# Compressed first-layer product of the second mixer on four column tiles, two chunks a step

## The reference, cut to what matters

```python
n_cmp = (T - CMP_LEN) // CMP_STRIDE + 1            # 15
blk = x[:, cmp_idx] + pe[None, None, :, None, :]
blk = jnp.transpose(blk, (0, 1, 3, 2, 4)).reshape(B, n_cmp, G, CMP_LEN * Dh)   # 2048 wide
hid = jax.nn.gelu(jnp.einsum('bngi,ih->bngh', blk, w1))                        # w1: 2048 x 256
return jnp.einsum('bngh,ho->bngo', hid, w2)                                    # w2: 256 x 64
```

## Time and profile before

| | us |
|---|---|
| median of 3 runs | 1629.38 |
| lowest, highest | 1627.42, 1630.9 |
| the profiled execution, its own time | 1627.93 |
| its span, first to last instruction | 1626.1 |
| PE busy in the span | 1592.5 |
| DVE busy | 951.4 |
| ACT busy | 802.6 |
| POOL busy | 167.1 |

### The profile page before, as it was taken

How to read it: one execution, slowest core, us unless ns; L and a number is a source line. 1 busy time by engine, 2 the same in 40 slices (tenths; PEclk the granted TensorE clock), 3 DMA queues, 4 the chain that set the end, 5 groups by cost and what they waited for, 6 DMA issues and landing times.

```text
span 1626.1 us, 22861 instructions
## 1 busy us (share of the span) xinstructions
PE 1592.5 (98%) x8768; PEld 1368.9 (84%) x8768; DVE 951.4 (59%) x1454; ACT 802.6 (49%) x1358; POOL 167.1 (10%) x187
## 2 busy tenths in 40 slices
PE   9999999999999999999999999999999989999997
PEld 7888899888888888888899988888888878878886
DVE  5555575444765555555456544665554778577865
ACT  6444465454364445444355454454443555453653
POOL 1000022211200000000022221120000301010100
PEclk9999999999999999999999999999999999999999
DMA  7665455443555554655546443446565453245421
GB/s 253 204 211 204 148 191 171 143 142 126 160 182 183 192 188 162 207 181 184 188 152 196 146 139 127 146 153 218 197 215 191 150 190 107 78 154 171 146 85 52
DMA packets 76718, 269.60 MB, mean 166 GB/s; under 512 B 8512, under 2 KB 9792, under 8 KB 76608
## 3 DMA queue, kind: packets, MB, share of 16 engines
q1 hardware_dynamic: 76320, 267.35, 49.4%
q10 hardware_dynamic: 288, 0.79, 0.1%
HBM read 267.06 MB, written 1.05 MB: 165 GB/s over the span
## 4 chain that ended last, share of the span: by engine, by line
PE 72%; DVE 5%; ACT 4%; issue 2%; POOL 1%; DMA 0%; POOLq 0%; DVEq 0%; ACTq 0%
PE bank L1433 20%; PE bank L1435 20%; PE bank L1434 20%; PE bank L1439 4%; PE bank L1558 2%; PE bank L1573 2%; DVE wlo L2281 1%; DVE cv L2278 1%; PE bank L1690 1%; ACT hh L1971 1%; ACT wk L2203 1%; PE bank L1500 1%; PE bank L1496 1%; PE bank L1492 1%; ACT whi L1968 1%
## 5 line engine op out<-in xcount | busy, mean ns | idle before, releaser
L2281 DVE TENSOR_TENSOR wlo<-raw,whi 128x1024 fp32r<-128x1024 f32 (+5 forms) x472 | 564.6, 1204 | 406.0 <-ACT whi L1968 370.4
L1968 ACT ACTIVATE whi<-raw 128x1024 fp32r<-128x1024 f32 (+4 forms) x500 | 508.9, 1029 | 426.4 <-PE bank L1435 394.6
L1433 PE MATMUL bank<-whi,hh 128*128 128x512 f32 (+3 forms) x1120 | 434.4, 388 | 0.0
L1435 PE MATMUL bank<-whi,hl 128*128 128x512 f32 (+3 forms) x1120 | 425.3, 380 | 0.0
L1434 PE MATMUL bank<-wlo,hh 128*128 128x512 f32 (+3 forms) x1120 | 424.8, 379 | 0.0
L1435 PEld LDWEIGHTS bank<-whi,hl 128*128 128x128 f32 x1120 | 210.5, 188 | 38.5
L1434 PEld LDWEIGHTS bank<-wlo,hh 128*128 128x128 f32 x1120 | 210.9, 188 | 35.9
L1433 PEld LDWEIGHTS bank<-whi,hh 128*128 128x128 f32 x1120 | 210.8, 188 | 35.6
L1433 PE MATMUL bank<-hh,whi 128*128 128x256 f32 x480 | 142.0, 296 | 0.0
L1433 PE MATMUL bank<-whi,gh 128*128 128x512 f32 x352 | 139.4, 396 | 0.0
L1435 PE MATMUL bank<-whi,gl 128*128 128x512 f32 x352 | 138.0, 392 | 0.0
(11 more groups left out here) (326 smaller groups left out, 1887.2 us busy)
## 6 DMA issues: line engine op xcount, KB each, us to landing
raw<-W SPq DMA_DIRECT2D x463, 512.0 KB, 3.3
raw<-W SPq DMA_DIRECT2D x26, 384.0 KB, 3.7
raw<-W SPq DMA_DIRECT2D x8, 416.0 KB, 3.0
tab<-tab SPq DMA_DIRECT2D x6, 384.0 KB, 4.0
raw<-W SPq DMA_DIRECT2D x4, 426.0 KB, 3.4
raw<-W SPq DMA_DIRECT2D x6, 192.0 KB, 2.6
x<-x_in SPq DMA_DIRECT2D x2, 512.0 KB, 6.5
tab<-gains SPq DMA_DIRECT2D x2, 512.0 KB, 4.9
```

What stands on the lines that cost most here:

```text
L1433: e.matmul(dst, ah, bh, start=start, stop=False)
L1435: return e.matmul(dst, al, bh, start=False, stop=stop)
L1968: return e.activation(dst, src, ACT.Copy)
L2281: return e.tensor_tensor(dst, src, hi.bitcast(F), ALU.subtract)
```

## The change

- `m2_cmp` takes two chunks a step. Each of a chunk's four slices goes to a column tile of its own, 32 columns of weights and all 256 hidden columns streaming. The tiles sum over different slices, so that PSUM holds 4 x 32 rows (four partial sums) x 256 per kv: a whole bank of 128 x 512.
- `m2_hid_copy` (new, on ACT) copies this bank to SBUF (`hid4`), and the bank is given back.
- `m2_hid_sum` (new, on PE): four f32 matmuls, with 128 columns of `hid4` as weights and a 128 x 30 matrix of zeros and ones (`K_SEL`) streaming. They add the four parts and turn the result at once, into 128 x 120.
- The gelu steps work on 128 x 120 rather than 64 x 256 and write `hid`; `m2_turn_hid` goes, and the factor 0.5 moves to the copy in `m2_cmp_out`.
- `tiles()` has four calls fewer, and the pace of `tick()` goes from 22/54 to 18/54.

```diff
-                for q in range(4):
-                    c = self.next("cmp")
-                    self.do("m2_cmp", l, c, kv, q, use)
-                    self.done(c)
+                for q in range(0, 4, 2):
+                    cs = [self.next("cmp") for _ in range(2)]
+                    self.do("m2_cmp", l, cs, kv, q, use)
+                    for c in cs:
+                        self.done(c)
                     yield
+            self.do("m2_hid_copy", l, use, base)
+            self.M2.give(use)
             told.add("hid")
-            self.hid = use
...
-            use = self.hid
-            yield
+            yield from pause(2)
+            use = self.M2.take()
+            self.do("m2_hid_sum", l, use)
+            yield from pause(2)
             self.do("m2_gelu_square", l, use, base)
...
-            yield from pause(5)
-            use = self.XB.take()
-            self.do("m2_turn_hid", l, use, base)
-            self.XB.give(use)
...
-            owed[0] += 22 / 54
+            owed[0] += 18 / 54
...
+    def m2_cmp(l, cs, kv, p, use):
+        bank = banks[use.i]
+        q.wait_ge(("blocks", l, kv), ("edge", l), use.before)
+        for n, c in enumerate(cs):
+            w = T.raw[c % NRAW]
+            q.wait_ge(("landed", c))
+            for k in range(4):
+                m = (p + n) * 4 + k
+                i = e.matmul(bank[32 * k:32 * k + 32, kv * 256:(kv + 1) * 256], T.bl32[:, kv, m * 30:m * 30 + 32],
+                             w[:, k * 256:(k + 1) * 256], start=p + n == 0, stop=p + n == 3)
+            i.then_inc(*q.tell("psum", ("used", c), *([use.full] if (kv, p + n) == (1, 3) else [])))
+
+    def m2_hid_sum(l, use):
+        q.wait_ge(("hid4", l), use.before, ("rest",))
+        for n in range(4):
+            i = e.matmul(banks[use.i][:, n * 30:(n + 1) * 30], T.hid4[:, tok(n)], T.kc[:, K_SEL:K_SEL + 30],
+                         start=True, stop=True)
+        i.then_inc(*q.tell("psum", use.full))
...
+    def m2_hid_copy(l, use, base):
+        q.wait_ge(use.full, base)
+        copy(T.hid4[:, :], banks[use.i][:, :]).then_inc(*q.tell("scal", ("hid4", l), use.free))
```

More of the change, by code:

```diff
@@ L1692, in m2_values @@
         i.then_inc(*q.tell("psum", u["p"].free, ("v_read", u["u"]), *([g["o"].full] if end else [])))
[L1694 to L1698, removed]
     def m2_cmp_out(l, use, base):
@@ L1756, in tensor @@
         m1_turn_heads, m1_scores, m1_turn, m1_values, m1_turn_group, m1_branch, m1_turn_merged, m2_decay_scan,
-        m2_turn_n, m2_cmp, m2_ln_mean, m2_ln_var, m2_ln_scale, m2_pw, m2_scores, m2_turn, m2_values, m2_turn_hid,
+        m2_turn_n, m2_cmp, m2_ln_mean, m2_ln_var, m2_ln_scale, m2_pw, m2_scores, m2_turn, m2_values, m2_hid_sum,
         m2_cmp_out, m2_turn_kc, m2_vbd, m2_cmp_scores, m2_turn_cmp, m2_cmp_values, m2_turn_nsa, m2_turn_fox)}
@@ L2211, in m2_turn @@
             *q.tell("scal", ("pt", u["u"], 0), use.free))
+    def m2_hid_copy(l, use, base):
+        q.wait_ge(use.full, base)
+        copy(T.hid4[:, :], banks[use.i][:, :]).then_inc(*q.tell("scal", ("hid4", l), use.free))
     def m2_gelu_square(l, use, base):
         q.wait_ge(use.full, base)
-        e.activation(T.hidr[:, :, :], banks[use.i][0:64, 0:256].rearrange("p (a b) -> p a b", a=2),
-                     ACT.Square).then_inc(*q.tell("scal", ("gelu_square", l)))
+        e.activation(T.hidr[:, :], banks[use.i][:, 0:120], ACT.Square).then_inc(*q.tell("scal", ("gelu_square", l)))
     def m2_gelu_tanh(l):
         q.wait_ge(("gelu_inner", l))
-        e.activation(T.hidr[:, :, :], T.hidr[:, :, :], ACT.Tanh).then_inc(*q.tell("scal", ("gelu_tanh", l)))
+        e.activation(T.hidr[:, :], T.hidr[:, :], ACT.Tanh).then_inc(*q.tell("scal", ("gelu_tanh", l)))
     def m2_turn_kc(l, use, base):
@@ L2699, in m2_gelu_inner @@
         q.wait_ge(("gelu_square", l))
-        e.tensor_scalar(T.hidr[:, :, :], T.hidr[:, :, :], 0.044715 * c, c, ALU.mult, ALU.add).then_inc(*q.tell("vec"))
+        e.tensor_scalar(T.hidr[:, :], T.hidr[:, :], 0.044715 * c, c, ALU.mult, ALU.add).then_inc(*q.tell("vec"))
         q.wait_ge(q.own("vec"))
-        e.tensor_tensor(T.hidr[:, :, :], T.hidr[:, :, :], hid_bank(use), ALU.mult).then_inc(
+        e.tensor_tensor(T.hidr[:, :], T.hidr[:, :], banks[use.i][:, 0:120], ALU.mult).then_inc(
             *q.tell("vec", ("gelu_inner", l)))
@@ L2706, in m2_gelu @@
         q.wait_ge(("gelu_tanh", l))
[L2707 to L2714, removed]
+        stt(T.hid[:, :, :].rearrange("p a b -> p (a b)"), T.hidr[:, :], 1.0, banks[use.i][:, 0:120], ALU.add,
+            ALU.mult).then_inc(*q.tell("vec", ("hid", l), use.free))
     def m2_cmp_out(l, use, base):
         q.wait_ge(use.full, base)
-        e.tensor_copy(T.kcv[:, :, :], banks[use.i][0:15, 0:256].rearrange("p (a b) -> p a b", a=2)).then_inc(
-            *q.tell("vec", ("kcv", l), use.free))
+        e.tensor_scalar(T.kcv[:, :, :], banks[use.i][0:15, 0:256].rearrange("p (a b) -> p a b", a=2), 0.5, None,
+                        ALU.mult).then_inc(*q.tell("vec", ("kcv", l), use.free))
     def m2_turn_kc(l, use, base):
@@ L2827, in vector @@
         m2_cg_gate, m2_ng, m2_ln_mean, m2_ln_var, m2_ln_scale, m2_silu_in, m2_silu, m2_conv_gate, m2_scores,
-        m2_nsa_group, m2_fox_group, m2_gelu_inner, m2_gelu, m2_turn_hid, m2_cmp_out, m2_turn_kc, m2_vbd, m2_cmp_scores,
+        m2_nsa_group, m2_fox_group, m2_gelu_inner, m2_gelu, m2_cmp_out, m2_turn_kc, m2_vbd, m2_cmp_scores,
         m2_cmp_max, m2_cmp_weights, m2_cmp_values, m2_nsa_gate, m2_turn_nsa, m2_fox_gate, m2_turn_fox, last, last_gain, last_half)}
@@ L2913, in constants @@
         kc[[h, 4 + h], K_FM + 7 + 2 * h] = 1
+    for p in range(128):
+        if p % 32 < 30:
+            kc[p, K_SEL + p % 32] = 1
     slopes = f(2.0) ** (f(-8.0) * np.arange(1, 19, dtype=f) / f(18))
```

11 lines of the change are left out of this document (5 added, 6 removed).

## The result

| | before | after |
|---|---|---|
| median, us | 1628.4 (4 runs) | 1650.86 (4 runs, 1650.1 to 1653.17) |
| profiled execution, its own time | 1627.93 | 1650.25 |
| its span | 1626.1 | 1648.5 |
| mean granted clock of PE | 0.994 | 0.983 |

The ratio is **1.0141, 95% interval [1.0128, 1.0153]**: 22 us slower. The direction was forecast, the size was not: 1635 was predicted, and the range ended at 1640.

The account below looks back on a forecast made before the run. PE was taken to bound nearly every stretch, though not the edited one throughout. Layer 0 +2.3, layer 1 +3.8 and ends 2 x 0.5 sum to +7.1 on 1627.93: 1635 us, range 1624 to 1640.

Parts of the forecast that it names:

- Items 1 and 2: Compressed product: four tiles side by side save 4.0 us of PE per layer; added and removed steps cost net +0.7.
- D: Rival: four column tiles run as two, some 0.7 us more per layer, about 1636.5; chance 0.04.
- Item 3: Layer 0, before the first half tile: weights must land earlier, PE idle some 2.6 us (2 to 3).
- Item 4: Layer 0, turn 1: ACT's in-order queue delays cumh; PE idle 3.4 us (2 to 4), balance 2.8 us late.
- The -0.5 behind turn 1: Layer 0, the turn after turn 1: the old wait of 0.57 us need not come again.
- item 6: Layer's end: W_out blocks still wait for ysl, +0.1; L1738 moves, +0.4; together +0.5 us per layer.
- Rival E: A half clock follows each new idle stretch of PE: +1.7 us per layer, 1638 to 1640; chance 0.09.
- A: Main case: stalls before chunk 8 and at turn 1 both stand, 1635 us; chance 0.48.
- C: Rival: neither stall, chunk 8 split before 1327.2, or both waits overstated by bookkeeping; about 1624; chance 0.17.
- B: Rival: the stall before chunk 8 stands, the one at turn 1 doesn't; even, about 1629; chance 0.22.

Follow-up runs that it names:

- e3_single: Changed kernel, kc 648 wide, with the old order (one chunk a step, pace 22/54), four-tile product, copy and sum kept; 1624.37 us, ratio 0.9983.
- e2_align: Changed kernel with constant tile kc 648 columns wide instead of 646; 1650.79 us, ratio 1.0143 to the kernel before.
- e5_pace: As e3_single (one chunk a step, four column tiles, kc 648 wide) but with pace 18/54 instead of 22/54; 1643.67 us, ratio 1.0096.
- e13_fill2: Changed kernel, kc 648 wide, unread matmuls filling PE's idle places ahead of chunks 4 to 7, first half tile, turns 1, 9, 18; 1653.94 us, ratio 1.0156.

## Why the prediction was right in sign and wrong in size

**Items 1 and 2, the product: right.** Sixteen records in 1.07 us, four tiles side by side; D falls. In the Trainium skill, "TensorE: Matmul & The Clock Gate" (Part 3, "What overlaps and what doesn't") has MATMULs start and end in program order. What falls is what the prediction made of that: an order of starts and ends doesn't keep matmuls on different tiles from overlapping. Predicted was -4.0 + 0.7 = -3.3 a layer; e3_single shows -3.0 and -2.7, with single chunks, though the time comes back at the layer's end and not at turn 1. That the sizes agree so well is in part luck. A single chunk holds PE for 1318.42 - 1317.85 = 0.57 us, two in a step for 1.00, so a switch of shapes costs 0.14 and pairs would save four of them, 0.6 a layer. The copy took 0.59 us of ACT, 0.6 predicted.

**Item 3, landings: right.** Counted back by the 5.1 us delay, chunk 4 is used at 1322.5 (1321.7 predicted as its landing), and the next ones about 1.4 us apart. The half tile starts at 1330.2 (1329.8 predicted), with 1.44 us idle and not 2.6, since PE had waited more on the single chunks ahead of it and ran chunks 6 and 7 and the scores at half clock.

**Item 4, ACT's order: right, 1 us short.** Softmax 0 ends 1333.6 (1332.7 predicted), cumh begins 1336.9 (1336.2), fb 1340.6 (1339.6), turn 1 1343.3 (1342.4), idle 3.07 (3.4). The balance is 4.2 us late and not 2.8. Of the 1.4 between them 0.9 is that date, and 0.5 is an error of the prediction's sum: it takes off the 0.7 of `m2_hid_sum` as work done ahead, which the old kernel never has to do; only the 0.2 of `m2_turn_hid` may be taken off. Put right, its own walk gives 3.3, and 4.8 in layer 1, where 5.4 was measured; the whole becomes 1636. The -0.5 behind turn 1 is near the 0.3 less of layer 0; layer 1 has 0.9 more.

**The step that failed: item 6, the layer's end.** It was set at +0.5 a layer, and +3.5 was measured in both. The item saw rightly that L1738 would leave its place, but gave it +0.4, as the cover of the wait for fql, and that wait is 0.65 then and now. What lost its cover was turn 18, which waits 2.04 for 0.20. The wait for ysl is 2.26, where that for oc was 2.00; +0.1 was predicted for this. And behind the new wait stand 3.4 us at half clock, 1.5 by the comparison above. 1.8 + 0.3 + 1.5 = 3.6. This is read from the traces of both kernels; no run changed turn 18's wait by itself.

**Rival E was not an alternative to A.** The prediction gave E 0.09 and left the clock out of the sum, but the idle time that A forecast is just what E needs. Where PE is the bound, each layer of the changed kernel has two stretches of 3.4 us at half clock more than the old one: the one behind turn 18, and one between turn 1 and turn 17 (in layer 0 the one from 1350.0, behind the 3.07 us of idle time). The 10.2 us at half clock from 1329.5 to 1339.8 were free. Between turn 1 and turn 17 the added stretch is in part balanced in layer 0 by shorter waits, 1.8 us in all for 2.7, though a new one stands at turn 9:

```profile
1379.78 0.44 PE L1440 MATMUL bank<-kc,wk 128*128 128x128 f32 x2 [1.31 <-ACT wk L1972]
```

In layer 1 the waits are 2.9 for 2.8. These are small terms beside what executions differ by: turn 17 of layer 0 stands at 99.4 in e2_align and at 96.8 in the changed kernel, which have the same order.

**The pace was priced nowhere.** The edit took 18/54 because `tiles()` has four calls fewer, and no item of the prediction gives the pace a price. e5_pace shows that it costs 18 us in itself where the steps stay single: it takes half tiles from between the turns and brings later those that others wait for.

**Not in the sum at all: 5.1 us ahead of the edited stretch**, 3.5 of it because 30 columns in a constant tile moved the feed-forward tiles, the other 1.6 with a longer half clock at the start of this execution:

```profile
8.60:15.40 6.80, 6.04 (x13) 0.50 0.77 284
```

**The rivals.** C said that the stalls may be an error of bookkeeping; they weren't. B fell with them. The test that the prediction set itself (half tile after 1328, turn 1 waiting over 2 us) came out for A, and still the time was 16 us off: the test looked only at the head of the layer. Of the 15.2 us that the span grew beyond the 7.1 predicted, 5.1 lie ahead, 2.5 at turn 1, 1.6 up to turn 17 and 6.0 at the ends.

Open: why the place of gh and gl matters, and how the 3.5 us of a layer's end divide between turn 18's wait and the clock behind it, which e13_fill2 was to give and didn't.

## What to carry to other kernels

Try a faster operation in the old order first; gathering its steps ahead of in-order queues is a second change with a price of its own, here 26 us against a gain of 6. Walk a changed order to the end of the stage and not to its first stall, count what each moved step had covered, take off as done ahead only what the other kernel still has to do, and let every forecast idle place bring its half clock where PE is the bound behind it. When a time is off, look first at stretches that were not edited: 30 columns in a shared constant tile cost 3.5 us a long way from the edit.

## What the runs showed of the hardware

- Four column tiles of an f32 product run side by side: 16 records of 256 columns in 1.07 us, as long as 16 of 128 columns on two tiles.
- The same feed-forward matmuls take 396 ns in place of 388 to 394 when their tiles gh and gl lie 120 bytes further in SBUF, without any wait and at full clock; those on bh and bl get faster by the same shift (wlo,bh 396 to 390).
- A half clock cost nothing where another engine set the date (25.91 us at 0.80, 25.69 at 1.00), and 1.5 us per stretch of 3.4 where PE did.
- Half the clock is not half the speed: a matmul of 512 columns (f32r) takes a step of 0.42 us at 0.50 and 0.23 at full clock, 1.8 times.
